# A hybrid attention, SSM and mLSTM block on one core: the first projection reads host-transposed x without its norm, and 1/rms is applied where the products are read

## The reference, cut to what matters

```
h    = rmsnorm(x, norm1_w)                       # x / rms(x) * w, one rms for each token
p    = h @ w_in                                  # 12 groups of 512 columns, and 24 narrow ones
xbc  = silu(causal_dwconv(p[xbc], 4 taps)); qk_m = silu(causal_dwconv(p[mqk], 4 taps))
dt   = softplus(p[dt] + bias); i, f = p[i] + bias, log_sigmoid(p[f] + bias)    # the narrow columns
att  = softmax attention of rmsnorm(q), rmsnorm(k), v
ssm  = mamba2 SSD(xbc, dt) gated by silu(z), normed; ml = chunkwise mLSTM(qk_m, v, i, f) gated by sigmoid(o)
x2   = x + concat(att, ssm, ml) @ w_out
out  = x2 + conv_glu(rmsnorm(x2, norm2_w))       # an up and a down projection with 11 steps
```

## Time and profile before

| | us |
|---|---|
| median of 3 runs (lowest, highest) | 426.46 (426.37, 426.61) |
| the profiled execution | 426.1 |
| its span, first to last instruction | 424.2 |

### The profile page before, as it was taken

How to read it: one execution, slowest core, us unless ns; L and a number is a source line. 1 busy time by engine, 2 the same in 40 slices (tenths; PEclk the granted TensorE clock), 3 DMA queues, 4 the chain that set the end, 5 groups by cost and what they waited for, 6 DMA issues and landing times.

```text
span 424.2 us, 6705 instructions
## 1 busy us (share of the span) xinstructions
PE 409.7 (97%) x2677; PEld 369.5 (87%) x2677; DVE 285.1 (67%) x399; ACT 245.6 (58%) x328; POOL 37.6 (9%) x28
## 2 busy tenths in 40 slices
PE   2999999999999999989999999999999999999996
PEld 2999999777888887767888999999999999999995
DVE  3889797756756688788545876575755655757663
ACT  4868877694378666888635564443554544435540
POOL 2522444410011000000000000000000000000000
PEclk9999999999999999999999999999999999999999
DMA  7754793445462432235544366445555454454202
GB/s 250 299 204 178 263 320 154 161 157 192 151 243 100 140 158 101 99 113 187 198 146 152 105 234 231 158 174 198 192 198 198 177 185 163 173 195 195 100 0 99
DMA packets 11581, 73.60 MB, mean 174 GB/s; under 512 B 1300, under 2 KB 1448, under 8 KB 3368
## 3 DMA queue, kind: packets, MB, share of 16 engines
q1 hardware_dynamic: 11560, 73.30, 47.8%
HBM read 72.23 MB, written 1.07 MB: 173 GB/s over the span
## 4 chain that ended last, share of the span: by engine, by line
PE 90%; ACT 5%; DMA 2%; DVE 2%; issue 0%; SPq 0%; ACTq 0%; DVEq 0%
PE pj L1191 23%; PE pj L1193 23%; PE pj L1192 23%; PE mx L1192 5%; PE mx L1191 5%; PE mx L1193 5%; PE mx L1245 5%; PE mx L1242 3%; DMA wraw<-in_w_in 2%; ACT whi L380 1%; ACT L508 1%; ACT seg_b L466 1%; DVE wlo L748 1%; ACT sz_b L508 0%; DVE xn L857 0%
## 5 line engine op out<-in xcount | busy, mean ns | idle before, releaser
L748 DVE TENSOR_TENSOR wlo<-wraw,whi 128x2048 fp32r<-128x2048 f32 x58 | 132.8, 2290 | 74.1 <-ACT whi L380 73.9
L380 ACT CAST whi<-wraw 128x2048 fp32r<-128x2048 f32 x63 | 119.7, 1903 | 75.7 <-PE pj L1193 75.7
L1191 PE MATMUL pj<-hT_hi,whi 128*128 128x256 f32 x512 | 145.4, 284 | 0.8 <-DVE hT_lo L767 0.8
L1193 PE MATMUL pj<-hT_hi,wlo 128*128 128x256 f32 x512 | 144.9, 283 | 0.0
L1192 PE MATMUL pj<-hT_lo,whi 128*128 128x256 f32 x512 | 144.9, 283 | 0.0
L1191 PEld LDWEIGHTS pj<-hT_hi,whi 128*128 128x128 f32 x512 | 98.0, 191 | 1.7 <-DVE hT_lo L767 1.0
L1192 PEld LDWEIGHTS pj<-hT_lo,whi 128*128 128x128 f32 x512 | 98.0, 191 | 0.4
L1193 PEld LDWEIGHTS pj<-hT_hi,wlo 128*128 128x128 f32 x512 | 98.0, 191 | 0.0
L1191 PE MATMUL pj<-whi,hT_hi 128*128 128x512 f32 x144 | 58.2, 404 | 0.0
L1193 PE MATMUL pj<-whi,hT_lo 128*128 128x512 f32 x144 | 56.3, 391 | 0.0
L1192 PE MATMUL pj<-wlo,hT_hi 128*128 128x512 f32 x144 | 56.1, 390 | 0.0
(11 more groups left out here) (210 smaller groups left out, 440.0 us busy)
## 6 DMA issues: line engine op xcount, KB each, us to landing
wraw<-in_w_in SPq DMA_DIRECT2D x23, 1024.0 KB, 4.8
wraw<-in_w_up SPq DMA_DIRECT2D x22, 1024.0 KB, 4.8
wraw<-in_w_down SPq DMA_DIRECT2D x11, 1024.0 KB, 4.8
wraw<-in_w_out SPq DMA_DIRECT2D x8, 1024.0 KB, 4.8
seg_b<-ld_rows SPq DMA_DIRECT2D x4, 512.0 KB, 5.8
x_sb<-in_x SPq DMA_DIRECT2D x2, 512.0 KB, 3.7
wraw<-in_w_in SPq DMA_DIRECT2D x4, 256.0 KB, 7.2
Wm_b<-m_rows_d SPq DMA_DIRECT2D x1, 512.0 KB, 6.8
```

Of the source, the lines that this page charges most:

```text
L380: nc.scalar.copy(whi[:, slot, :], wraw[:, slot, :]).then_inc(s.hi_done, 1)
L748: nc.vector.tensor_tensor(wlo[:, slot, :], wraw[:, slot, :], whi[:, slot, :].bitcast(F32), ALU.subtract).then_inc(s.lo_done, 1)
L1191: pe_mm(ps, a_hi, b_hi, start=start, stop=False, skip_group_check=shared)
L1193: return pe_mm(ps, a_lo, b_hi, start=False, stop=stop, skip_group_check=shared)
```

## The change

- The host adds norm1_w and x in transposed form (`xt`, 1 MB and 4 KB), loaded first, in three pieces between the four pieces of unit 0. ACT and VectorE make `hT_hi` and `hT_lo` from it directly, with norm1_w as scale and without 1/rms. The 16 transposes and the scaled rows are gone. x in token rows is loaded behind unit 2, the parameters and the narrow weights behind unit 3, each ahead of the next unit.
- Units 0, 1 and 2 are split in four pieces each, all on ACT and VectorE. `POOL_UNITS` becomes 4, 5, 6, 8, 9, 10, 12.
- 1/rms is made behind all these pieces, spread over the partitions by two matmuls inside unit 2 (`spread_r1`) and kept in `rbc`.
- New `conv_scale(g)` on VectorE: two instructions read `pj`, multiply by `rbc` and write `cg` in SBUF. `conv_base` and `conv_taps` read `cg`; TensorE may reuse `pj` after `conv_scale`.
- The narrow products are multiplied by `rbc` first. `small_proj` moves to slot 2; `rows_softplus` and `rows_scans` to slot 3, `rows_dec` to slot 4 (behind the taps of group 1), `cols_turn` to slot 5.
- The evictions of v, o, z and the squares of q and k take 1/rms as ACT's scale, one instruction for each half of the tokens in place of one for both.

The diff, cut to its core:

```
-    POOL_UNITS = (4, 6, 8, 10, 12)
+    POOL_UNITS = (4, 5, 6, 8, 9, 10, 12)
+        cg = so_b[:, :].rearrange("p (k t) -> p k t", k=4)
...
+            sp.dma_start(xn_b[:, 0:a], A["xt"][:, 0:a]).then_inc(s.xt_in0, 16)
+            load_first(0)
+            sp.dma_start(xn_b[:, a:b], A["xt"][:, a:b]).then_inc(s.xt_in1, 16)
+            load_first(1)
+            load_first(2)
+            sp.dma_start(xn_b[:, b:], A["xt"][:, b:]).then_inc(s.xt_in2, 16)
+            load_first(3)
+            for u in range(1, U_OUT):
+                if u == 3:
+                    sp.dma_start(x_sb[:, 0, :], A["x"][0, 0:P, :]).then_inc(s.x_in0, 16)
+                    sp.dma_start(x_sb[:, 1, :], A["x"][0, P:T, :]).then_inc(s.x_in1, 16)
+                if u == 4:
                     sp.dma_start(par[:, :], A["par"][:, :]).then_inc(s.par_in, 16)
+                    sp.dma_start(w24, A["w24"].rearrange("p (k n) -> p k n", k=KD)).then_inc(s.w24_in, 16)
                 slot_free(u)
...
-                group_computed(g)
+                act.wait_ge(s.conv_in, 2 * g + b + 1)
...
-                    nc.scalar.activation(acc[:, b, i, :], pj[g % 2][:, k * T:(k + 1) * T], ACT.Identity,
+                    nc.scalar.activation(acc[:, b, i, :], cg[:, k, :], ACT.Identity,
...
+                for c in range(NT):
+                    nc.scalar.activation(sz[:, c, i * GC:(i + 1) * GC], pj[(G_Z + i) % 2][:, c * 512:(c + 1) * 512], ACT.Silu,
+                                         scale=rstd(c)).then_inc(s.z_ready, 1)
...
+            def conv_scale(g):
+
+                dve.wait_ge(s.unit_done, 2 * g + 2)
+                if g:
+                    dve.wait_ge(s.conv_done, 2 * g)
+                for b in range(2):
+                    nc.vector.tensor_tensor(cg[:, 2 * b:2 * b + 2, :], pj[g % 2][:, 512 * b:512 * (b + 1)].rearrange("p (k t) -> p k t", k=2),
+                                            rbc[:, :].unsqueeze(1).to_broadcast([P, 2, T]), ALU.mult).then_inc(s.conv_in, 1)
...
-                        ins = nc.vector.scalar_tensor_tensor(out=acc[:, b, i, back:T], in0=pj[g % 2][:, k * T:(k + 1) * T - back],
+                        ins = nc.vector.scalar_tensor_tensor(out=acc[:, b, i, back:T], in0=cg[:, k, 0:T - back],
...
-            at(0, rows_softplus)
+            at(3, rows_softplus)
+            at(3, rows_scans)
+            first_at(1, conv_scale, 0)
             for g in range(NCONV):
+                if g:
+                    at(2 * g + 2, conv_scale, g)
                 for b in range(2):
                     at(2 * g + 2, conv_taps, g, b)
-            at(2, rows_scans)
-            at(3, rows_dec)
+            at(4, rows_dec)
...
-            at(0, small_proj)
-            at(4, cols_turn)
+            at(2, small_proj)
+            at(5, cols_turn)
...
-            read_by = [(s.conv_done, 2 * g + 2) for g in range(NCONV)] + [
+            read_by = [(s.conv_in, 2 * g + 2) for g in range(NCONV)] + [
```

More of the change, by code:

```diff
@@ L934, in qk_scale @@
                 link(nc.vector.reciprocal(r, r))
+                for c in range(NT):
+                    h = slice(c * AH, (c + 1) * AH)
+                    mark(nc.vector.tensor_scalar(r[:, h], r[:, h], stat[:, 2 + c:3 + c], None, ALU.mult))
+                settled()
                 nc.vector.tensor_tensor(qk_rows[:, i, :].rearrange("p (a d) -> p a d", d=DH),
@@ L1193, in products, with first_unit, channels_first @@
                 return pe_mm(ps, a_lo, b_hi, start=False, stop=stop, skip_group_check=shared)
[L1195 removed]
+            def first_unit(ps):
+                for k in range(4):
+                    pe.wait_ge(s.hi_T, k + 1)
+                    pe.wait_ge(s.w0_hi, k + 1)
+                    for c in range(4):
+                        nc.tensor.matmul(ps[:, c * T:(c + 1) * T], whi[:, 0, k * 512 + c * P:k * 512 + (c + 1) * P], hT_hi[:, k, :],
+                                         start=k == 0 and c % 2 == 0, stop=False, skip_group_check=True)
+                    pe.wait_ge(s.lo_T, k + 1)
+                    for c in range(4):
+                        nc.tensor.matmul(ps[:, c * T:(c + 1) * T], whi[:, 0, k * 512 + c * P:k * 512 + (c + 1) * P], hT_lo[:, k, :],
+                                         start=False, stop=False, skip_group_check=True)
+                    pe.wait_ge(s.w0_lo, k + 1)
+                    for c in range(4):
+                        ins = nc.tensor.matmul(ps[:, c * T:(c + 1) * T], wlo[:, 0, k * 512 + c * P:k * 512 + (c + 1) * P], hT_hi[:, k, :],
+                                               start=False, stop=False, skip_group_check=True)
+                return ins
+            def channels_first(ps, slot, half, turned=None, pieces=None, between=None, where=2):
                 for k in range(4):
                     kk = half * 4 + k
[L1199 removed]
+                    if k == where and between:
                         between()
@@ L1256, in turn_rows, with spread_r1 @@
                             ins.then_inc(ps_sem, 1)
+            def spread_r1():
+                pe.wait_ge(s.consts, 4)
+                pe.wait_ge(s.rd1_ready, NT)
+                for t in range(NT):
+                    ins = mm(bank[1][:, t * P:(t + 1) * P], ones[:, :], rdiag[:, t, :])
+                ins.then_inc(s.rb1_ps, 1)
             def small_proj():
@@ L1482, in _ @@
                     pe.wait_ge(*read_by[g - 2])
-                if u >= 2:
+                kind = channels_first if g < NCONV else tokens_first
+                if u == 0:
+                    first_unit(pj[0]).then_inc(s.unit_done, 1)
+                elif u == 1:
+                    channels_first(pj[0], 1, 1, s.lo_T, s.w1_lo).then_inc(s.unit_done, 1)
+                elif u == 2:
+                    channels_first(pj[1], 2, 0, pieces=s.w2_lo, between=spread_r1, where=1).then_inc(s.unit_done, 1)
+                else:
                     lo_ready(pe, u)
-                kind = channels_first if g < NCONV else tokens_first
-                if g == 0:
-                    channels_first(pj[0], u, half, s.lo_T, (s.w0_lo, s.w1_lo)[u]).then_inc(s.unit_done, 1)
-                else:
                     kind(pj[g % 2], u % NR, half).then_inc(s.unit_done, 1)
```

184 lines of the change are left out of this document (98 added, 86 removed).

## The result

| | before | after |
|---|---|---|
| median, us (lowest, highest) | 426.41 (426.31, 426.61) | 449.31 (449.05, 449.60) |
| the profiled execution | 426.1 | 449.05 |
| its span | 424.2 | 447.2 |

The account below looks back on a forecast made before the run. TensorE was taken to bound the kernel before, with VectorE's queue, blocked by GpSimd splits, delaying it after: 426.1 + 24.3 (shift at `kt`) + 0.2 (z) = 450.6 us, median 451.0, range 428 to 456.

Parts of the forecast that it names:

- The gain at the start: On TensorE, an earlier start ends units 3 to 5 at 47.3 against 49.6 before, a gain of 2.3 us.
- its own upper case: Whole kernel: weights 2 us later and one more blocked split or two slow clock restarts (3.2 us) give 457 us.
- The landing of unit 4: Weights of unit 4 land at 24.8 us, slow early transfers counted once; 22.8 without them, 26.8 counted twice.
- Rival (c): No contention and no loss in early transfers: unit 4's weights land at 22.8, total 425.0 us; chance 0.05.
- The exclusion of the taps: VectorE taps with two SBUF inputs wait for GpSimd splits, up to 4.6 us; total 451.0 us, chance 0.67.
- Rival (a): Only tensor_tensor is blocked, adding 3.3 us in the scans; unit 6 at 54.0, total 430.3 us; chance 0.15.
- rival (b): No contention reaches the path: unit 6 at 50.7, 0.3 late, total 427.0 us; chance 0.09.
- Turns between the two engines: Group 0: GpSimd splits to 31.6, one tap to 32.1, next split to 36.7, 11 taps to 41.5 us.
- The scan: GpSimd's split of unit 6 runs 48.4 to 53.0 inside VectorE's scans; the other scans end at 56.0 us.
- The shift at `kt`: `st_copy` starts at 109.1, 84.8 before; nothing changes from there to `kt`, so the shift is 24.3 us.
- a slow restart of the clock twice (3.2): TensorE's matmuls run slowly when restarting, 1.6 us each time; two restarts, 3.2 us, counted only toward the upper end.
- z: TensorE's wait for z, now read in two halves, grows by 0.1 us for each of two groups: 0.2.

Follow-up runs that it names:

- taps_psum: Changed kernel with the scaled product written back into `pj` in PSUM, where base and taps read it: 435.84 us, ratio 1.0215 to the kernel before.
- before_copy: Kernel before the change, plus only a VectorE copy of each group's product to SBUF, from which base and taps read: 438.08 us.
- the finer splits: Changed kernel with each GpSimd split cut in four instructions of 512 columns: 447.43 us.
- reordered: hybrid with half of unit 5's split on VectorE, `cols_copy` between the halves of group 1's taps, `bc_copy` ahead of `conv_base(4)`: 429.25 us, ratio 1.0069.
- psum_order_pool: psum_order with unit 6 split by VectorE instead of GpSimd: 432.19 us, ratio 1.0129 to the kernel before.
- warm_psum: psum_order_pool with idle TensorE products, 8 ahead of `cols_turn` and 34 behind it: 430.01 us against 432.19 without.
- psum_order: taps_psum with `rows_exps` ahead of group 1's base and `rows_dec` ahead of group 1's taps: 434.83 us, ratio 1.0191 to the kernel before.
- hybrid: psum_order_pool with group 1's scaled product alone in SBUF (`cg`) and `rows_dec` ahead of `conv_scale(1)`: 429.52 us, ratio 1.0074 to the kernel before.

## Why the prediction was right

451.0 was predicted, 449.3 measured, by the mechanism that the prediction named. Step by step:

| step, us | predicted | measured |
|---|---|---|
| first matmul | 5 to 8 | 5.45 |
| unit 2 done | 27.0 | 26.70 |
| unit 4's weights | 24.8 | 24.54 |
| GpSimd done with units 4, 5 | 36.7 | 35.90 |
| taps of group 0 done | 41.5 | 40.62 |
| GpSimd's split of unit 6 | 48.4 to 53.0 | 46.77 to 51.26 |
| scans done | 56.0 | 54.50 |
| `cols_turn`, and the wait ahead of it | 63.2, 15.9 | 61.83, 14.9 |
| taps of groups 2, 3, 4 done | 80.1, 96.2, 108.5 | 78.36, 94.41, 106.57 |
| wait before `state` | about 7 | 6.1 |
| `st_copy` | 109.1 | 107.14 |
| shift at `kt` | 24.3 | 22.6 |

- *The gain at the start* came as worked out: unit 2 was done 0.3 earlier than forecast, and all of the gain went into the wait at `cols_turn`. The 0.3 is a slip of the sum: 13.3 + 0.6 + 0.7 is 14.6 and not 14.9, and unit 1 began at 14.67. In the same way GpSimd's split of unit 6 should have stood at 47.7 - 1.5 + 1.9 = 48.1 and not 48.4, and the range ends at 456 where its own upper case gives 457. None of this touches the mechanism.
- *The landing of unit 4* was taken with the slow early transfers counted once, which held to 0.3, but par's small lines are not their cause: par comes late now, and the window from 5 to 6 us still moved 174 GB/s. Rival (c) falls with it.
- *The exclusion of the taps* is shown, by `taps_psum` (same order, other memory, 13.5 us), by `before_copy` and by the finer splits. Rival (a), that only tensor_tensor waits, is refuted by the scan (4.74) and the taps (4.83 the longest); rival (b) by the same rows. The rule of the Trainium skill in "SBUF — State Buffer", section "Who interferes with whom", for two SBUF inputs holds here for scalar_tensor_tensor and for a scan on 16 partitions as well.
- *Turns between the two engines*, that one tap gets in between two GpSimd splits, was the step with least ground, and the rows of group 0 show it: the first tap ended at 31.42, 0.3 behind the first split; the second tap, begun at 31.35, ended at 36.18, 0.3 behind the second. Its cost was taken too high. The tap that got in held the second split up by 0.2 (4.80 for 4.6) and not by 0.5, so GpSimd was done at 35.90 for 36.7 predicted and the taps at 40.62 for 41.5.
- *The scan* met GpSimd's split of unit 6 as forecast: they began within 0.02 us of each other, and it waited for all of it. The taps of group 1 ran free (5.31), as in the sum.
- *The shift at `kt`* was right in size and in the path that it named, but this path is not alone. I put the shift down to `st_copy`, "from it to `kt` nothing changes". The chain that ended last does not go through `st_copy`. It goes through `state`, 81.66 before and 102.51 after, 20.9 late, and then along TensorE. The rows of that chain, start, length, what:

```profile
102.51 3.78 PE mx L1316 x4
106.29 0.43 PE pj L1248
...
108.45 0.23 PE pj L1248
...
112.56 1.72 PE mx L1316 x4
```

  `state` took 3.78 for the 1.88 of before, and the matmuls behind it 0.43 for 0.23 until 108: the clock had fallen in the 6.1 us wait. That is 2.6 us, and `inter` begins at 112.40 for 88.88 before, 23.5 late. But `kt` also needs `inter_evac`'s addition on VectorE, and this ended at 119.33, only 0.3 ahead of `kt`. Two rows of the way to it, on ACT and on VectorE:

```profile
112.66 1.90 ACT L390 CAST whi<-wraw 128x2048 fp32r<-128x2048 f32 x1 [0.74 <-PE pj L1250]
```
```profile
118.11 1.22 DVE L896 TENSOR_TENSOR xn_b<-xn_b,xw_b 128x1024 f32<-128x1024 f32 x1
```

  From `st_copy` (107.14, 22.4 later than before) to the end of the addition it is 12.2 us, 12.0 before. ACT's split waited 0.7 for the slow TensorE, and the addition took 1.22 for 1.94, because this time it began 0.02 ahead of the GpSimd instruction that had blocked it. So the two ways to `kt` are almost equally long. At full clock the way along TensorE would be 2.6 shorter and the way through `st_copy` 0.7, so the slow clock cost `kt` some 0.7 to 0.8, an estimate from these rows, and not 2.6; the prediction had called the clock cheap and kept it only as an end of its range ("a slow restart of the clock twice (3.2)"). That the addition gave as much back was luck. What is left of the difference between 24.3 and 22.6 is VectorE's queue, which was 1.9 ahead of what I had worked out by the end of the taps of group 4.
- *z* grew by 0.2 for one group, 1.7 for 1.5, and not twice: predicted 0.2 for two.
- *What the forecast did not see* is L805, the tensor_scalar from SBUF to SBUF. It cost nothing, because it came behind GpSimd's pair; in `taps_psum` and the versions built on it, it cost 2.5 to 2.7, until `reordered` halved the second split. Of the scan the forecast was right that it is blocked, though which of the two engines began first was a matter of 0.02 us.

## What to carry to other kernels

Before an operand is moved from PSUM to SBUF for the sake of an early release, list what GpSimd runs beside its readers: every VectorE instruction that then reads SBUF twice can wait for a whole GpSimd instruction, here up to 4.8 us for one that takes 0.48. A wait that is removed is worth only what the next one in the queue leaves, so follow the in-order queue of the busiest helper engine to the second and third place where TensorE needs it. A long wait of TensorE (4.7 us in `psum_order_pool`, 3.0 in `reordered`) costs more than its length where TensorE is late, since the matmuls behind it ran at half the clock for some 3 to 5 us.

## What the runs showed of the hardware that I had not expected

- A tensor_scalar of 16 partitions x 256 elements, SBUF to SBUF, waited for GpSimd: 2.83 us in `taps_psum` and `warm_psum`, 3.03 in `psum_order`, 3.06 in `psum_order_pool`, 2.90 in `hybrid`, and 0.34 in the changed kernel, where GpSimd had ended. It has one tensor input only, and beside it a bias of one value a partition (`par`); which of the two reads makes it wait no run parts. That it read faster from SBUF (0.34) than the same form from PSUM (0.47) fits the Trainium skill, "VectorE: DVE Perf Modes", section "Mode 2×_2P — use both read ports for one tensor": a one-source operation between SBUF tensors uses the second port too. The same form from PSUM beside a GpSimd split was not tried; a copy of 128 x 512 elements from PSUM was, in `before_copy`, and its two copies at 29.66, both beside a split, took 0.69 and 0.68 us, and such a copy begun at 45.25, away from any split, 0.67.
- A small instruction is blocked as long as a large one: a scan of 16 x 128 elements, 0.41 us by itself, waited 4.3 us (4.4 in `taps_psum`).
- The granted clock fell to 0.50 in the waits of 14.9 and 6.1 us of the changed kernel, 4.7 of `psum_order_pool` and 3.0 of `reordered`. In `psum_order_pool` it still shows 0.88 over 50 to 54 us, most of the wait; behind the wait it shows 0.50 from 54 to 59 and 0.58 from 59 to 60. Behind the wait of 2.5 us in `hybrid`, which ended at 57, the windows show 1.00.
- PEclk does not show the slow start. It reads 1.00 over the first 16 transposes of the kernel before, which took 3.36 us where 16 of the same form took 1.91 at 56.05, so the 1.00 that the prediction read there doesn't tell the clock.
- The first MB arrive slowly even where par's small lines are not among them: in the changed kernel 174 and 270 GB/s between 5 and 7 us, 389 from 7 to 8. The cause stays open.
